# Hybrid trunk kernel: how the input rows are loaded and first transposed, and where one weight load stands in the queue

## The reference, cut to what matters

```python
xn = _rmsnorm(h, norm_mix[l])
proj = xn @ w_in[l]                       # q | k | v | u, 512 columns each
y_a = _dilated_attention(q, k, v, rel_bias)
y_b = _s5_mixer(u, ...)                   # diagonal state recurrence on u
h = h + concat(rmsnorm(y_a), rmsnorm(y_b)) @ w_out[l]
h = h + _memory_attention(_rmsnorm(h), _rmsnorm(mem), ...)
h = h + _moe(_rmsnorm(h), ...)            # top 4 of 32 experts
return _rmsnorm(h, norm_final)
```

## Time and profile before

| | us |
|---|---|
| median of 3 runs | 2411.97 |
| lowest and highest | 2409.12, 2412.51 |
| profiled execution, its own time | 2411.03 |
| span of its profile | 2409.0 |
| PE busy in the span | 2278.1 (95%) |

### The profile page before, as it was taken

How to read it: one execution, slowest core, us unless ns; L and a number is a source line. 1 busy time by engine, 2 the same in 40 slices (tenths; PEclk the granted TensorE clock), 3 DMA queues, 4 the chain that set the end, 5 groups by cost and what they waited for, 6 DMA issues and landing times.

```text
span 2409.0 us, 34021 instructions
## 1 busy us (share of the span) xinstructions
PE 2278.1 (95%) x13746; PEld 1772.3 (74%) x13747; DVE 661.9 (27%) x1677; ACT 304.8 (13%) x652; POOL 571.9 (24%) x1157
## 2 busy tenths in 40 slices
PE   7999998898979599999999999999999999999996
PEld 4546545644455378498989899898898988988975
DVE  2132237323255522122222222122222222222213
ACT  3002035211141100000000000000001000000002
POOL 3714885002003421111111211201112012112102
PEclk9999998999999799999999999999999999999998
DMA  8614210620002595898687888888989899999985
GB/s 204 120 63 46 58 30 2 178 88 35 5 10 97 192 360 193 299 370 264 217 274 259 291 276 281 283 269 281 301 262 299 272 309 294 297 321 295 304 294 167
DMA packets 442564, 509.41 MB, mean 211 GB/s; under 512 B 52261, under 2 KB 369029, under 8 KB 442404
## 3 DMA queue, kind: packets, MB, share of 16 engines
q1 hardware_dynamic: 427192, 470.16, 59.7%
q0 software_dynamic: 13648, 35.93, 6.1%
q10 hardware_dynamic: 1564, 1.10, 0.2%
HBM read 470.88 MB, written 38.54 MB: 211 GB/s over the span
## 4 chain that ended last, share of the span: by engine, by line
PE 76%; DVE 1%; issue 1%; ACT 1%; POOL 1%; DMA 0%; ACTq 0%; POOLq 0%; DVEq 0%
PE ps L2317 40%; PE ps L2332 11%; PE ps L2240 10%; PE ps L1240 8%; PE ps L1616 2%; PE ps L2219 1%; PE ps L2272 1%; ACT px L1450 1%; PE ps L1254 1%; PE ps L1637 0%; POOL table_dram L1821 0%; DVE px L1395 0%; POOL rs L295 0%; DVE negx L1385 0%; PE ps L1247 0%
## 5 line engine op out<-in xcount | busy, mean ns | idle before, releaser
L2317 PE MATMUL ps<-xT,we 128*128 128x128 f32 (+10 forms) x7680 | 980.9, 290 | 13.3 <-issue 13.3
L2317 PEld LDWEIGHTS ps<-xT,we 128*128 128x128 f32 x7680 | 970.1, 191 | 28.0 <-issue 21.4
L2460 DVE TENSOR_SCALAR glu<-ps,b1s 128x128 f32<-128x128 f32 (+10 forms) x240 | 89.0, 371 | 961.9 <-PE ps L2317 959.6
L2113 POOL DMA_INDIRECT xg<-xn_dram,gx x148 | 153.7, 1038 | 482.5 <-DVE xT L2425 442.4
L2332 PE MATMUL ps<-actT,we 128*128 128x160 f32 (+9 forms) x1792 | 261.1, 307 | 0.0
L2332 PEld LDWEIGHTS ps<-actT,we 128*128 128x128 f32 x1792 | 253.8, 190 | 5.6 <-DVE outT L2486 2.1
L2240 PE MATMUL ps<-we,actT 128*128 128x512 f32 (+1 forms) x576 | 238.2, 595 | 0.7 <-ACT actT L2635 0.7
L2611 ACT ACTIVATE sg<-glu 128x256 f32<-128x256 f32 (+10 forms) x122 | 55.0, 451 | 1202.4 <-DVE glu L2460 1131.9
L2132 POOL DMA_INDIRECT acc_dram<-orow,sx x43 | 67.3, 1564 | 584.0 <-ACT orow L2599 426.3
L2240 PEld LDWEIGHTS ps<-we,actT 128*128 128x128 f32 (+1 forms) x576 | 100.4, 184 | 136.6 <-issue 135.7
L803 PE MATMUL ps<-xnT,wa 128*128 128x512 f32 x384 | 167.8, 598 | 7.9 <-DMA wa<-in_w_in 7.9
(11 more groups left out here) (347 smaller groups left out, 1772.7 us busy)
## 6 DMA issues: line engine op xcount, KB each, us to landing
we<-in_w SPq DMA_DIRECT2D x384, 1024.0 KB
wa<-in_w_in SPq DMA_DIRECT2D x4, 2048.0 KB, 12.5
acc_dram<-h SPq DMA_DIRECT2D x10, 512.0 KB, 2.6
xrow<-in_x SPq DMA_DIRECT2D x32, 128.0 KB, 6.1
wa<-in_w_xkv SPq DMA_DIRECT2D x2, 2048.0 KB, 9.9
h<-in_x SPq DMA_DIRECT2D x4, 1024.0 KB, 20.5
fin<-acc_dram SPq DMA_DIRECT2D x8, 512.0 KB, 5.3
out<-fin SPq DMA_DIRECT2D x32, 128.0 KB, 2.4
```

Source lines behind the costliest of these rows:

```text
L2113: pool.indirect_dma_start(xg[q % 2][:, b, :], None, xn_quarters, bass.IndirectOffsetOnAxis(m.gx[:, s % 3, half, b:b + 1], 0), bounds_check ...
L2317: last = nc.tensor.matmul(bank[:, part * WIN:part * WIN + W], view[:, k, (j % 2) * P:(j % 2 + 1) * P], m.xT[:, k, 0:W], start=(k == 0), st ...
L2460: v.tensor_scalar(m.glu[:, b, i * WIN:i * WIN + C], bank[:, 0:C], m.b1s[:, col, j:j + 1], LIMIT, ALU.add, ALU.min).then_inc(glu_ok, 1)
```

## The change

Each block of 128 rows comes by one DMA whose DRAM side is viewed as (g, i, d), that is 4 by 32 by 1024, and whose SBUF side is the 128 partitions of the tile; `g_mix` is issued after block 0. The first half is transposed block by block: for each block two groups of four transposes, chunks 0 to 3 and 4 to 7, each copied by DVE in one `tensor_tensor` with the gain broadcast along the tokens. ACT copies nothing of the first half and squares all eight blocks in a row. The first product goes ahead of `rsb_(0)`. `weights_in(3)` and its wait stand ahead of the wait for `u_out` and the 8 reads of `U`. The mapping of rows to partitions is unchanged.

```diff
     for half in range(2):
-        for k in range(KC):
-            plan(("x", half, k), "act" if k % 2 == 0 else "dve")
+        for n in range(8):
+            plan(("x", half, n), "dve" if half == 0 or n % 2 else "act")
...
         def rows_in(b):
-            for g in range(4):
-                sp.dma_start(m.xrow[32 * g:32 * g + 32, b], a.x[b * P:(b + 1) * P].rearrange("(i g) d -> g i d", g=4)[g]).then_inc(x_in[b], 16)
+            sp.dma_start(m.xrow[:, b], a.x[b * P:(b + 1) * P].rearrange("(i g) d -> g i d", g=4)).then_inc(x_in[b], 16)
...
-        for b in range(4):
+        rows_in(0)
+        sp.dma_start(m.g_mix[:], a.norm_mix.rearrange("(k p) -> p k", p=P)).then_inc(mix_in, 16)
+        for b in range(1, 4):
             rows_in(b)
-        sp.dma_start(m.g_mix[:], a.norm_mix.rearrange("(k p) -> p k", p=P)).then_inc(mix_in, 16)
         weights_in(0)
...
+        sp.wait_ge(p_full, VM0)
+        weights_in(3)
         sp.wait_ge(u_out, 16)
         for s in range(T):
             sp.dma_start(m.U[s * CH:(s + 1) * CH], a.u_dram[:, s * J:(s + 1) * J].rearrange("(g c) j -> c g j", c=CH)).then_inc(U_in, 16)
-        sp.wait_ge(p_full, VM0)
-        weights_in(3)
...
         for half in range(2):
             for b in range(4 * half, 4 * half + 4):
-                act.wait_ge(x_in[b], 64)
+                act.wait_ge(x_in[b], 16)
                 square(b, m.xrow[:, b])
-            if half == 0:
-                act.wait_ge(mix_in, 16)
-            for k in range(0, KC, 2):
-                x_out(half, k)
+        act.wait_ge(mix_in, 16)
+        for k in range(0, KC, 2):
+            x_out(1, k)
...
-        for k in range(1, KC, 2):
-            x_out(0, k)
+        for b in range(4):
+            for q in range(2):
+                g = at[("x", 0, 2 * b + q)]
+                dve.wait_ge(t_full, g + 1)
+                nc.vector.tensor_tensor(m.xnT[:, 4 * q:4 * q + 4, b * P:(b + 1) * P], t_bank(g).rearrange("p (k t) -> p k t", t=P),
+                                        m.g_mix[:, 4 * q:4 * q + 4].unsqueeze(2).to_broadcast([P, 4, P]), ALU.mult).then_inc(t_dve, 1)
...
+        def x_blocks():
+            for b in range(4):
+                pe.wait_ge(x_in[b], 16)
+                for q in range(2):
+                    transposes([m.xrow[:, b, (4 * q + i) * P:(4 * q + i + 1) * P] for i in range(4)])
...
         pe.wait_ge(ident_ok, 3)
-        x_in_(0)
+        x_blocks()
+        pe.wait_ge(wa_in[0], 16)
+        t_copied(pe, at[("x", 0, 7)])
+        by_weights(0, 0, 0)
         rsb_(0)
-        pe.wait_ge(wa_in[0], 16)
-        for k in (6, 7):
-            t_copied(pe, at[("x", 0, k)])
-        by_weights(0, 0, 0)
```

More of the change, by code:

```diff
@@ L808, in by_weights, with x_second @@
             project(lambda k: weights_of(n)[:, k, c * P:(c + 1) * P], lambda k: m.xnT[:, k, half * 512:(half + 1) * 512], 512)
-        def x_in_(half):
-            for b in range(4 * half, 4 * half + 4):
-                pe.wait_ge(x_in[b], 64)
+        def x_blocks():
[3 more added lines that the diff above has]
+                    transposes([m.xrow[:, b, (4 * q + i) * P:(4 * q + i + 1) * P] for i in range(4)])
+        def x_second():
+            for b in range(4, NB):
+                pe.wait_ge(x_in[b], 16)
             for k in range(KC):
-                transposes([m.xrow[:, 4 * half + i, k * P:(k + 1) * P] for i in range(4)])
+                transposes([m.xrow[:, 4 + i, k * P:(k + 1) * P] for i in range(4)])
         def rsb_(half):
@@ L831, in _ @@
             put(lambda out: nc.tensor.matmul(out[0:H_A, 0:hi - lo], m.rb[:], m.ohb[:, lo:hi], start=True, stop=True))
-        x_in_(1)
+        x_second()
         by_weights(0, 1, 0)
```

## The result

The changed kernel takes 2425.64 us in the median of 6 runs (2419.3 to 2429.0), the kernel before 2410.55 in 6 runs beside it (2403.0 to 2413.18). The ratio is 1.0064 with a 95% interval of 1.0043 to 1.0084: slower by 15 us, where 2427 and 15.3 us were forecast. The profiled execution has a span of 2427.0 against 2409.0; its own time, 2429.0, is the longest of the six, so the traces show a larger difference (18.0) than the medians.

The account below looks back on a forecast made before the run. PE, busy 95% of the span, was taken as the bound, so its idle or slow time decides. 25.0 us lost at the start less 9.7 gained gives 15.3, 2427 us against the median; range 2418 to 2453, likeliest case 2421 to 2432.

Parts of the forecast that it names:

- Which engines carry the rows: Row loads at the start: outermost dimension 4 against 128 confines each transfer to four DMA engines, 97 GB/s together.
- Price of a block: Row loads at the start: 5.4 us a block, four engines at 24.3 GB/s each; bounds 5.0 to 5.8.
- Rival A: Row loads: four engines in each other's way, 8.4 us a block, block 7 at 78.2, time 2451 us; chance 0.29.
- What stands between: Queue between row blocks: g_mix 1 us, first weights' share 5.4 us; block 3 at 27.2, weights 32.6, block 7 54.2.
- The slow clock: Second half's transposes: after 9 us idle they take 6.54 us, not 3.71, 2.8 us more; start loses 25.0 us.
- The k weights: PE's second stop: issued at 103.3, landing about 114; 7.91 us of stop and 1.79 of slow clock go, 9.7 gained.
- a shift of PE passes to the end whole: PE from about 35 or 117 us on: everything behind is tied to its progress, so a shift reaches the end undiminished.
- Transposes by block: First half's start: first product could move up by up to 6 us if rows and weights came no later.
- Rival B: Row loads: all 16 engines carry them, 1.35 us a block, first product near 16.4, time 2397 us; chance 0.16.
- Sum: Whole kernel: 25.0 us lost at the start less 9.7 gained at the k weights is 15.3 us slower, 2427 us.

Follow-up runs that it names:

- e4: Changed kernel with each block's rows loaded in plain order, 128 outermost on both sides; only the start is read, first product at 14.98 us, whole time 3229.74 us.
- e5: Changed kernel with each block's rows in two transfers, each viewed as 2 by 32 by 1024 to 64 partitions; 2456.81 us in one run.
- e6: Changed kernel with the load of g_mix issued by ACT behind the one-hot table, not by SP between blocks 0 and 1; 2420.68 us, ratio 1.0062.
- e1: Kernel before with only the one transfer per block, transposes and order of all else as before; 2433.3 us, ratio 1.0106.
- e2: Kernel before with only the load of the k weights moved ahead of the 8 reads of U; 2401.21 us, ratio 0.9975.
- e3: Changed kernel with its one transfer per block put back to four of 32 partitions; 2400.14 us, ratio 0.9973.
- e7: e2 with two of each first-half block's four row transfers issued by ACT, so two groups of 32 partitions are in flight; 2395.29 us, ratio 0.9957.

## Why the prediction was right, step by step

**Which engines carry the rows.** Right, and it decided the sign: share 0.26, 105 GB/s, and with 2, 4 and 128 outermost entries 2, 4 and 16 engines (after, e4, e5). The Trainium skill (DMA: Bandwidth & Descriptors, the section on why a DMA increments its semaphore by 16) has the engine count as the largest number up to 16 that divides the slowest dimension of both sides. The traces agree. With the advice of the same page (Rules for kernel authors) to use one 128-partition transfer in place of two for parts, they agree only in e4, where both sides have 128 outermost (408 to 420 GB/s against the 250 of the kernel before); in the changed kernel the one transfer has 105.

**Price of a block.** 5.4 us was forecast, at 24.3 GB/s an engine; undisturbed it is 4.9 to 5.1, at 26. Rival A, 8.4 us, is out: four engines side by side don't slow each other, for with two (e5), four (24 to 28 us) and sixteen (e4, 16 to 18 us) a 4 KB packet takes 159 ns.

**What stands between.** Here a term was missing. The sum gave blocks 1 to 3 three times 5.4 us and 1 for `g_mix`, 17.2 us; by the measured price of a block they would need 15.3. They took 20.6 (9.79 to 30.34). Most of the 5 us more fall where the first weights run on the other engines, which the sum held to be without effect (the packets under e6, and e1). Some 1.4 us are lost before that: from 4 to 12 us the changed kernel moves 88 and then 73 GB/s, e1, where `g_mix` stands behind block 3, 95 and 104. `g_mix` on the way may explain a part; in e5 it costs 0.3 us. The rest is open. The errors partly cancel, a block price that was too high against the missing term: block 3 at 30.3 for 27.2, the weights at 35.5 for 32.6, block 7 at 55.6 for 54.2. That the last is only 1.4 us off is in part luck. What exactly the weights share with the row transfers (ports, memory) was not tried.

**The slow clock.** The second half's transposes took 6.40 us, forecast 6.54: 2.7 us more than before, forecast 2.8. The start lost 26.6 us, forecast 25.0.

**The k weights.** Right: 7.9 us of stop and 1.9 of low clock are gone, 9.7 us at that place in e2 and 10.0 in the changed kernel. They landed 8.3 us after issue, not 10.7, which changed nothing, for PE asked 13.5 us after issue. The step behind it, that a shift of PE passes to the end whole, does not hold as it stands. In e2 8.1 us are left at the products of q and 3.5 at L1647, and its median is 6 us lower, not 9.7 (2 to 10). In the changed kernel the group on `U` takes 3.24 us instead of 2.56. The idle 4.88 us before that group was seen, but not that its after-effect on the clock differs: over all the traces the group takes 2.56 to 3.75 us.

**Transposes by block.** The sum gave them no gain with slow rows. Rival B's terms held in e4 (weights at 15.0, forecast 16.4; a low clock at the first product, 9.76 us, 2.7 more where 1.8 was allowed; the second half's transposes 4.2 us earlier than before, forecast 5). With rows at the old rate nothing is left of that: in e3 the same transposes start 1.5 us later. Two small things were off and cost nothing: the change saves 24 issues (32 to 8), not 28, and the 8 transposes of a block take 1.97 us, not 1.6.

**Sum.** By the traces 26.6 lost less 10.0 gained is 16.6 us at 203.57, and 18.0 at the end of the span; the forecast has 15.3, the medians 15.1 (10 to 20). The mechanism was right. That the medians agree to 0.2 us is luck: the traces show terms that were 1.6 us off in the start alone, and the stretch from q to L1647 took anything from 596 (e6) to 607 us (e2) with the same work.

## What to carry to other kernels

Before merging several transfers into one, look at the outermost dimension of both sides of the merged view: fewer issues don't matter if the transfer then runs on 4 of 16 DMA engines. Here it was the DRAM side's dimension that was small (2, 4), while the SBUF side had 64 or 128 partitions. The DMA share of a window with nothing else in flight gives the number of engines away: 0.26 is four, 0.13 is two. And an earlier start of TensorE by short bursts between waits is worth little if the product behind it then runs at the low clock: the first product took 8.6 to 10.0 us so, 1.6 to 3.0 more than its 7.03.

## What the runs showed of the hardware that was not expected

SP's own issues were held up where four engines carried the queue: the small load of `lam` took 14.51 us to issue in the changed kernel, 3.37 before. Blocks 4 to 7 stood behind it, and yet it cost nothing that can be seen: the four engines never ran dry, 103 to 108 GB/s in every window of 4 us from 24 to 52.

Two queues that write different groups of 32 partitions lift the rate of the rows: 298 GB/s at 4 to 8 us in e7, where one queue had 244 in the same window of the kernel before. It stays below the 408 to 420 of e4.
